# The order of the 64-row products in a gated-linear-attention layer: heads and chunks alternate on the TensorE array

## The chip, the cores and the metric

The kernel runs on one core of a Trainium2 chip. The metric is the device time of one execution in microseconds; lower is better. Three timed runs of the kernel before gave 604.95, 606.73 and 607.09 us (median 606.73). All views below come from one further execution, recorded by the hardware profiler.

## What is computed

One step of a hybrid block: adaLN-RMSNorm, a mixer with two branches (a gated linear recurrence, RG-LRU, and gated linear attention, GLA), a projection and residual, then a hierarchical mixture of 16 experts and a last norm. There are 640 tokens (512 latent ones, 128 of the prompt), 1024 channels, all in float32. The change touches the GLA part, which the reference writes as follows (4 heads of 64 key rows and 128 value columns, chunks of 64 tokens, a forward and a backward direction):

```python
def gla_scan(q, k, v, logg, s0):
    ...
    att = jnp.einsum('bhnid,bhnjd->bhnij', q * jnp.exp(b - b_ref), k * jnp.exp(b_ref - b))
    att = jnp.where(mask, att, 0.0)
    o_intra = jnp.einsum('bhnij,bhnjv->bhniv', att, v)
    q_in = q * jnp.exp(b)
    kv = jnp.einsum('bhnjd,bhnjv->bhndv', k * jnp.exp(b_last - b), v)
    decay = jnp.exp(b_last[:, :, :, 0, :])
    def step(s, inp):
        q_c, kv_c, d_c = inp
        o = jnp.einsum('bhid,bhdv->bhiv', q_c, s)
        return d_c[..., None] * s + kv_c, o
    ...
```

Three kinds of product come from it: the scores (`att`), the chunk states (`kv`) and the read-out (`o_intra` plus `o_inter`).

## The kernel before

Every engine has its own instruction list, written out by hand and tied together by semaphores; TensorE's list is the block under `@block.tensor`. Its results go to PSUM. Three places of 1024 floats (two banks each) form a ring, `ps`; each product takes the next place in a fixed list, `order`, and may start only when the product three places earlier has been taken out of PSUM by its reader. This wait is the last line of `start(name)` (L1098): `wait_taken(pe, ring[n - RING])`. `order` also names the reader of each product, A for ScalarE and D for VectorE, who serve them in that order; a second pair of banks, `ms`, holds products that stand aside from the ring, among them the turned keys `kT`.

Around the change TensorE does, for each of four groups g (a group is a direction s = g % 2 and a pair of heads tt = g // 2, which lie in the upper and the lower 64 rows of a tile):

- `kT{g}` (L1263): five transposes of the decayed keys, waiting for `kd_ready`.
- `at{g}0` and `at{g}1` (L1272), the scores of the two heads: for each of five 128-token tiles one product with 64 rows (the head's half of the rows, `rows_h`) and 128x128 outputs. The two heads go into two places of the ring. The change is here.
- `og{g}` (L1104, `project`), the first half of a 1024-deep projection to 128 x 640, which waits for its 512 KB tile of weights.
- `kvA{g}` and `kvB{g}` (L1291), the chunk states: products with 64 rows (the half that holds the chunk) and 64 output rows (the head), 20 in all, in which chunk and head alternate.
- the second half of `og{g}`.

In ring order this is at{g}0, at{g}1, og{g}, kvA{g}, kvB{g}, and again for g + 1. So at{g+1}0 takes the place of og{g}, which ScalarE empties (L897), and at{g+1}1 the place of kvA{g}, which VectorE empties. VectorE's list has, for each g: `scores(g)`, which takes both heads' scores through a mask (L1756; for odd g L1759 adds them to the sum of both directions); for g = 0 and 1 also `differences(g + 2)` (L1737, L1738) and `scale_qk(g + 2)` (L1743, L1744), with ScalarE's exponentials (L919 to L923) between them; then `carry(g)`, which runs the recurrence over the chunks of kvA (L1774, seven steps) and of kvB (L1782, L1783).

Then comes the read-out. TensorE does yl0, attend(0), yl1, attend(1), turn_o(0), yl2, attend(2), turn_o(1), yl3, attend(3), turn_o(2), attend(4), turn_o(3). `attend(t)` makes the 128 x 512 output of token tile t. For each head: one product of the scores with the values, with 128 rows and 128 columns (L1312), and up to four products of `qin` with the chunk states, with 64 rows (the head's half) and 64 output rows (the half of the chunk's tokens), for two chunks and two directions (L1322). The heads of a pair write into different banks (`hh * 512`). Tile 4 has two L1322 products per head, the others four. ScalarE takes the squares of each o{t} (L999) and their roots (L1001), VectorE the reciprocal and the scaling (L1815, L1820), TensorE turns the result (L1330, `turn_o`), and VectorE gates it (L1825). Between them ScalarE takes yl{t} through a gelu (L990). After that follow the output projection `mix` (L1386), the router and the experts (L1453, L1474).

Of the kernel before, what the change touches and what calls it, by code (L numbers as in the profile page):

```python
# [12 lines left out]
P = 128  # L13
EPS = 1e-6
GRID_W = 64
CHUNK = 64
# [4 lines left out]
def hybrid_step(nc, x_prompt, x_sample, state_lru, state_gla, c, c_ctx, ada_w, ada_b, norm1_g, w_in,  # L21
# [8 lines left out]
    NT = N // P  # L30
# [4 lines left out]
    HEADS, DK, DV = state_gla.shape[3:]  # L35
# [3 lines left out]
    NC = N // CHUNK  # L39
    SC = NS // CHUNK  # L40
# [22 lines left out]
    with ctx:  # L63
        def sb(name, shape, dt=F32):
            return ctx.enter_context(nc.sbuf_tensor(name, shape, dt))

        def sem(name):
            return ctx.enter_context(nc.semaphore(name))
# [14 lines left out]
        v = vtok[:, :].rearrange("p (t n) -> p t n", t=NT)  # L83
# [20 lines left out]
        qin = bcum  # L104
        softp = mixT[:, LC:, :]
        gt = tmp[:, 0:6 * N].rearrange("p (j n) -> p j n", j=6)
        attb = tmp[:, 6 * N:7 * N]
        att = tmp[:, 8 * N:12 * N].rearrange("p (h n) -> p h n", h=HEADS)
        o0 = 12 * N + LC * XLP
        NST = 8  # L110
        S = tmp[:, o0:o0 + 4 * NST * DV].rearrange("p (g c v) -> p g c v", g=4, c=NST)
# [7 lines left out]
        def state_slot(s, cn):  # L119

            return NST - 1 if cn >= SC else cn - 1 if s == 0 else cn
# [44 lines left out]
        sg0 = sb("sg0", [P, 4, DV])  # L166
# [126 lines left out]


        made = {name: n + 1 for n, (name, _) in enumerate(order)}
        for g in range(4):
            at_og = made[f"og{g}"]
# [10 lines left out]
        def product(name):  # L308
            if name in turned_keys:
                return ms[:, :, :].rearrange("p b n -> p (b n)")  # L310
            return ms[:, aside[name], :] if name in aside else ps[:, place[name] % RING, :]
# [20 lines left out]
        def weights(name):  # L332
            return wring[:, slot_of[name], :].rearrange("p (k n) -> p k n", k=KD)
# [21 lines left out]
        product_ready = sem("product_ready")  # L355
# [86 lines left out]
        at, off = [], 0  # L442
        for _, n in sm_parts:
            at.append(off)
            off += n
# [10 lines left out]
        def wait_tile(eng, name, i):  # L456
            eng.wait_ge(tile_in[i], 16 * (tiled[name][1] + 1))

        def count(name):

            n = [m for m, _ in order].index(name)
            who = order[n][1]
            return who, sum(w == who for _, w in order[:n + 1])

        def wait_taken(eng, name):
            who, n = count(name)
            eng.wait_ge(took[who], n)
# [615 lines left out]
        def _(pe):  # L1083
            mm = nc.tensor.matmul

            def start(name):

                if name in turned_keys:
                    wait_taken(pe, f"kT{int(name[2:]) - 1}" if name != "kT0" else "aTx")
                    return product(name)  # L1090
                if name in aside:
                    same = [m for m in aside if aside[m] == aside[name]]
                    if same.index(name):
                        wait_taken(pe, same[same.index(name) - 1])
                    return product(name)
                n = place[name]
                if n >= RING:
                    wait_taken(pe, ring[n - RING])  # L1098
                return product(name)
# [60 lines left out]
            def project(name, w, col, ks=range(KD)):  # L1160

                dst = start(name)
                for k in ks:
                    i = wide(dst, w[:, k, col:col + P], hT[:, k, :], k == 0, k == KD - 1)
                if k == KD - 1:
                    i.then_inc(product_ready, 1)
# [52 lines left out]
            dst = start("gd")  # L1219
            for k in range(KD):  # L1220
                r = 32 * (k % 4)
                for d, x in zip(halves(dst), halves(hT[:, k, :])):
                    i = mm(d[r:r + 2 * RANK, :], wgd[:, k, :], x, start=(k < 4), stop=(k >= 4), skip_group_check=True)
# [33 lines left out]
            for g in range(4):  # L1257
                r = 3 * (g % 2)
                tt = g // 2
                pe.wait_ge(kd_ready, g + 1)  # L1260
                dst = start(f"kT{g}")
                for t in range(NT):
                    i = nc.tensor.transpose(dst[:, t * P:(t + 1) * P], gt[:, r + 2, t * P:(t + 1) * P], ident[:, :])  # L1263
                i.then_inc(product_ready, 1)

                pe.wait_ge(qk_ready, g + 1)
                for hh in range(2):
                    dst = start(f"at{g}{hh}")
                    rows_h = slice(hh * DK, (hh + 1) * DK)
                    for t in range(NT):  # L1270
                        cols = slice(t * P, (t + 1) * P)
                        i = mm(dst[:, cols], gt[rows_h, r + 1, cols], gt[rows_h, r, cols], start=True, stop=True)  # L1272
                    i.then_inc(product_ready, 1)

                wait_tile(pe, "og", g)
                project(f"og{g}", weights("og"), g * P, range(0, KD // 2))
                wait_taken(pe, f"kT{g}")
                if g == 3:
                    pe.wait_ge(mod_out, 3)
                    nc.tensor.transpose(ms[0:8 * KD, 0, 0:P], A2[:, :, :].rearrange("p a k -> p (a k)"), ident[:, :]).then_inc(rowsT, 1)  # L1280
                    pe.wait_ge(lfin_ready, 8)
                    nc.tensor.transpose(ms[0:8, 0, P:2 * P], lfin[:, :], ident[:, :]).then_inc(lfinT, 1)
                for name, chunks in ((f"kvA{g}", range(SC)), (f"kvB{g}", range(SC, NC))):
                    dst = start(name)
                    for cn in chunks:
                        half = slice((cn % 2) * CHUNK, (cn % 2 + 1) * CHUNK)
                        col = (cn % 2) * 512 + (cn - chunks[0]) // 2 * DV
                        t = cn // 2
                        for hh in range(2):
                            h = 2 * tt + hh  # L1290
                            i = mm(dst[hh * DK:(hh + 1) * DK, col:col + DV],  # L1291
                                   kdT[g % 2][half, t * P + hh * DK:t * P + (hh + 1) * DK], v[half, t, h * DV:(h + 1) * DV],
                                   start=True, stop=True)
                    i.then_inc(product_ready, 1)
                project(f"og{g}", weights("og"), g * P, range(KD // 2, KD))
# [8 lines left out]
            def attend(t):  # L1304
                dst = start(f"o{t}")
                cols = slice(t * P, (t + 1) * P)
                for h in range(HEADS):
                    tt, hh = h // 2, h % 2
                    rows_h = slice(hh * DK, (hh + 1) * DK)

                    out = slice(hh * 512 + tt * DV, hh * 512 + (tt + 1) * DV)
                    mm(dst[:, out], att[:, h, cols], v[:, t, h * DV:(h + 1) * DV], start=True, stop=False, skip_group_check=True)  # L1312
                    parts = []
                    for cn in (2 * t, 2 * t + 1):
                        for s in range(2):
                            if cn >= SC and cn == (SC if s == 0 else NC - 1):
                                continue
                            first = cn == (0 if s == 0 else SC - 1)
                            parts.append((cn, s, sg0[rows_h, 2 * tt + s, :] if first else S[rows_h, 2 * tt + s, state_slot(s, cn), :]))
                    for n, (cn, s, state) in enumerate(parts):  # L1320
                        r = (cn % 2) * CHUNK
                        i = mm(dst[r:r + CHUNK, out], qin[rows_h, 2 * tt + s, cn * CHUNK:(cn + 1) * CHUNK], state, start=False,  # L1322
                               stop=(n == len(parts) - 1), skip_group_check=True)
                i.then_inc(product_ready, 1)

            def turn_o(t):
# [6 lines left out]
            for t in range(4):  # L1333
                if t:
                    wait_tile(pe, "yl", t)
                    project(f"yl{t}", weights("yl"), t * P)
                attend(t)
                if t:
                    turn_o(t - 1)
            attend(4)  # L1340
            turn_o(3)

# [81 lines left out]
            for n in range(2 * NT):  # L1424
                i = mm(ms[:, 0, 288:288 + 2 * NE], sel_a[:, n // NT, n % NT, :],  # L1425
                       gate_sel[:, n // NT, n % NT, :, :].rearrange("p h e -> p (h e)"), start=(n == 0),
                       stop=(n == 2 * NT - 1), skip_group_check=True)
# [65 lines left out]
            with pe.If(n_over > 0):  # L1493
# [4 lines left out]
                with pe.Fori(0, NOV) as i:  # L1498
                    with pe.If(n_over > i):
# [14 lines left out]
                        for half in range(2):  # L1514
                            for k in range(DC):
                                m = mm(ps[:, 2, half * 512:(half + 1) * 512], aT[:, 0, k, :], e2[0][:, k, half * 512:(half + 1) * 512],
                                       start=(k == 0), stop=(k == DC - 1))
# [686 lines left out]
```

## Time and profile before

| | |
|---|---|
| median of 3 runs | 606.73 us (604.95 to 607.09) |
| the profiled execution: its time | 606.16 us |
| its span, first to last instruction | 604.3 us |
| mean granted TensorE clock | 0.975 |
| TensorE busy | 554.6 us, 92% of the span |
| VectorE, ScalarE, GpSimd busy | 49%, 34%, 17% |
| scores (L1272) | 80 records, 187.1 to 230.3 us |
| read-out (L1312, L1322) | 40 and 144 records, 250.7 to 296.8 us |

Times inside the span count from its start. PE is TensorE's matmuls, PEld its weight loads, DVE VectorE, ACT ScalarE, POOL GpSimd, SP the queue that issues most transfers. A float32 product is recorded as two matmuls and two weight loads: the 40 score products stand as 80 records. A matmul's recorded duration contains its way through the array, so that neighbours overlap; the distance of starts, or the time that a chain gives to a run of them, is what a product costs.

### The profile page before, as it was taken

The numbers are of one execution on the slowest core, as the hardware profiler recorded it, in microseconds if no ns is written. First come the engines' busy times: TensorE is split into PE (matmuls) and PEld (weight loads), VectorE is DVE, ScalarE is ACT, GpSimd is POOL, SyncE is SP. The second block draws the span as 40 slices with busy tenths as digits, with TensorE's granted clock in tenths as the row PEclk, the third lists the DMA queues.
The fourth block names the chain that finished last, engine by engine and source line by source line (L and its number), as shares of the span: only waits on it lengthen the run. The fifth ranks groups of instructions, "written<-read, shape, count | busy, mean of one in ns | idle before, by whom it ended". The sixth has DMA issues, their size and how long they took to land.

```text
span 604.3 us, 6409 instructions
## 1 busy us (share of the span) xinstructions
PE 554.6 (92%) x2358; PEld 298.7 (49%) x2358; DVE 298.7 (49%) x592; ACT 203.3 (34%) x372; POOL 103.3 (17%) x113
## 2 busy tenths in 40 slices
PE   0899999999999999999999999699999999999970
PEld 0445545554346665566545555464454454454430
DVE  0532646948303764021344455515765576666671
ACT  5422289972412201533411122210000543443440
POOL 3000000001501220000000000040232454453332
PEclk9999999999999999999999999769999999999995
DMA  7977664118537802600019511179999999999411
GB/s 278 387 239 205 207 203 145 36 35 285 183 124 187 283 1 73 193 0 1 1 26 390 211 69 70 70 241 398 398 364 361 349 331 358 348 324 337 165 49 47
DMA packets 74418, 120.44 MB, mean 199 GB/s; under 512 B 13890, under 2 KB 31635, under 8 KB 74387
## 3 DMA queue, kind: packets, MB, share of 16 engines
q1 hardware_dynamic: 63880, 104.23, 49.7%
q0 software_dynamic: 10368, 15.75, 7.3%
q8 instruction: 19, 0.31, 0.2%
q14 instruction: 13, 0.10, 0.0%
q10 hardware_dynamic: 138, 0.04, 0.0%
HBM read 115.51 MB, written 26.51 MB: 235 GB/s over the span
## 4 chain that ended last, share of the span: by engine, by line
PE 85%; ACT 4%; DVE 3%; issue 1%; DMA 1%; POOL 0%; POOLq 0%; DVEq 0%
PE ps L1104 25%; PE ms L1453 18%; PE ps L1386 12%; PE ps L1474 9%; PE ps L1179 6%; PE ps L1436 2%; PE ps L1124 2%; PE ps L1322 2%; PE ms L1124 1%; PE ps L1272 1%; PE ms L1357 1%; PE ps L1312 1%; PE ps L1291 1%; PE ms L1425 1%; DMA wring<-in_w_in_dram 1%
## 5 line engine op out<-in xcount | busy, mean ns | idle before, releaser
L1104 PE MATMUL ps<-r,wring 128*128 128x512 f32 (+1 forms) x512 | 143.7, 436 | 1.6 <-ACT mixT L897 0.9
L1104 PEld LDWEIGHTS ps<-r,wring 128*128 128x128 f32 x512 | 79.0, 191 | 67.3 <-issue 66.1
L1386 PE MATMUL ps<-wring,mixT 128*128 128x512 f32 x160 | 72.1, 599 | 0.5 <-DVE tmp L1865 0.5
L1453 PE MATMUL ms<-wring,tmp 128*128 128x512 f32 x128 | 57.7, 593 | 1.3 <-DVE tmp L2044 1.3
L684 POOL DMA_INDIRECT mixT<-h_rows,slot_tok x16 | 19.6, 1224 | 192.6 <-DVE slot_tok L1972 178.8
L1386 PEld LDWEIGHTS ps<-wring,mixT 128*128 128x128 f32 x160 | 29.2, 190 | 32.0 <-issue 31.3
L1453 PEld LDWEIGHTS ms<-wring,tmp 128*128 128x128 f32 x128 | 23.6, 190 | 27.9 <-issue 26.3
L1179 PE MATMUL ps<-wring,r 128*128 128x512 f32 x80 | 35.6, 598 | 0.5 <-issue 0.5
L1043 ACT ACTIVATE tmp<-ms 128x256 f32<-128x256 f32 x16 | 6.1, 384 | 88.6 <-PE ms L1453 88.6
L2079 DVE TENSOR_TENSOR tmp<-ps,tmp 128x512 f32<-128x512 f32 x32 | 22.1, 691 | 16.8 <-PE ps L1474 16.8
L1453 PE MATMUL ms<-r,tmp 128*128 128x512 f32 x64 | 30.1, 617 | 0.0
L1054 ACT ACTIVATE tmp<-xres 128x512 f32<-128x512 f32 x24 | 15.1, 630 | 41.2 <-DVE xres L2083 41.2
L1453 PE MATMUL ms<-tmp 128*128 128x512 f32 x64 | 28.8, 592 | 0.0
L1474 PE MATMUL ps<-wring,gd 128*128 128x512 f32 x64 | 28.8, 592 | 0.0
L700 POOL DMA_INDIRECT residual_rows<-xres,back_row x16 | 16.4, 1024 | 69.4 <-DVE xres L2083 69.1
L1016 ACT ACTIVATE gd<-xres 128x512 f32<-128x512 f32 x10 | 6.3, 630 | 59.5 <-DVE xres L1869 59.5
L1179 PEld LDWEIGHTS ps<-wring,r 128*128 128x128 f32 x80 | 14.8, 190 | 19.9 <-issue 19.8
L2044 DVE COPY tmp<-ps 128x1024 f32<-128x1024 f32 x15 | 18.4, 1224 | 9.9 <-PE ps L1436 9.5
L2083 DVE TENSOR_TENSOR xres<-xres,tmp 128x512 f32<-128x512 f32 x32 | 22.1, 692 | 1.1
L2059 DVE COPY gd<-ps 128x256 f32<-128x256 f32 x16 | 6.8, 424 | 27.9 <-PE ps L1463 27.9
L2072 DVE SCALAR_TENSOR_TENSOR tmp<-qk,tmp 128x1024 f32<-128x1024 f32 x16 | 20.4, 1275 | 0.0
L1830 DVE TENSOR_TENSOR mixT<-mixT,gd 128x640 f32<-128x640 f32 x4 | 3.3, 825 | 34.5 <-ACT gd L990 34.5
(318 smaller groups left out, 825.1 us busy)
## 6 DMA issues: line engine op xcount, KB each, us to landing
wring<-in_ada_w_dram SPq DMA_DIRECT2D x12, 2048.0 KB, 11.9
wring<-in_exp_w_dram SPq DMA_DIRECT2D x8, 2048.0 KB, 24.8
wring<-in_w_in_dram SPq DMA_DIRECT2D x16, 512.0 KB, 4.9
r<-in_exp_w_dram SPq DMA_DIRECT2D x4, 2048.0 KB, 22.5
wring<-in_exp_w_dram SPq DMA_DIRECT2D x8, 1024.0 KB, 18.8
tmp<-in_exp_w_dram SPq DMA_DIRECT2D x4, 2048.0 KB, 22.5
wring<-in_w_out_dram SPq DMA_DIRECT2D x2, 2048.0 KB, 12.3
vtok<-in_exp_w_dram SPq DMA_DIRECT2D x4, 1024.0 KB, 17.0
```

Source lines behind the costliest of these rows:

```text
L684: pool.indirect_dma_start(gx[:, b, :], None, h2_d[:, :], rows_at(slot_tok[:, e:e + 1]), bounds_check=N - 1, oob_is_err=False).then_inc(gx_ ...
L700: pool.indirect_dma_start(xacc_d[:, :], rows_at(back_row[:, e:e + 1]), xr[:, u % 3, :], None, bounds_check=N - 1, oob_is_err=False).then_i ...
L1104: i = mm(d, lhsT, r, start=first, stop=last)
L1124: i = mm(dst[r:r + 32, 0:512], vec[:, k, :], w[:, k, :], start=(k < 4), stop=(k >= 4), skip_group_check=True)
L1179: i = mm(dst[:, 0:512], hT[:, k, t * P:(t + 1) * P], w[:, k, :], start=(k == 0), stop=(k == KD - 1))
L1386: i = mm(product(f"mx{t}")[:, half * 512:(half + 1) * 512], mixT[:, k, t * P:(t + 1) * P], w[:, k, :], start=(k == 0), stop=(k == KD - 1))
L1453: i = mm(ms[:, b, :], xgT[:, b, k, :], e13[u % 4][:, k, :], start=(k == 0), stop=(k == KD - 1))
L1474: i = mm(ps[:, 2, half * 512:(half + 1) * 512], aT[:, b, k, :], e2[u % 4][:, k, half * 512:(half + 1) * 512], start=(k == 0), stop=(k == D ...
L2044: V.tensor_copy(xgT[:, u % 2, :, :].rearrange("p k n -> p (k n)"), ps[:, 0, :]).then_inc(x_taken, 1)
L2072: link(stt(g2, rows[1][3], prompt[:, e:e + 1], rows[0][3], ALU.mult, ALU.add))
L2079: tt_(g2[:, cols], ps[:, 2, cols], g2[:, cols], ALU.mult).then_inc(y_taken, 1)
L2083: tt_(xr[:, u % 3, cols], xr[:, u % 3, cols], g2[:, cols], ALU.add).then_inc(z_half, 1)
```

## The change

In the scores both places of the ring are asked for first, then the two heads alternate from tile to tile. In the read-out the two heads of a pair go together: both 128-row products first, then for each direction and chunk the product of one head and that of the other. The number, sizes and operands of the products stay the same.

```diff
@@ -1264,13 +1264,15 @@
                 pe.wait_ge(qk_ready, g + 1)
-                for hh in range(2):
-                    dst = start(f"at{g}{hh}")
-                    rows_h = slice(hh * DK, (hh + 1) * DK)
-                    for t in range(NT):
-                        cols = slice(t * P, (t + 1) * P)
-                        i = mm(dst[:, cols], gt[rows_h, r + 1, cols], gt[rows_h, r, cols], start=True, stop=True)
-                    i.then_inc(product_ready, 1)
+
+                dsts = [start(f"at{g}{hh}") for hh in range(2)]
+                for t in range(NT):
+                    cols = slice(t * P, (t + 1) * P)
+                    for hh in range(2):
+                        rows_h = slice(hh * DK, (hh + 1) * DK)
+                        i = mm(dsts[hh][:, cols], gt[rows_h, r + 1, cols], gt[rows_h, r, cols], start=True, stop=True)
+                        if t == NT - 1:
+                            i.then_inc(product_ready, 1)
@@ -1304,23 +1306,23 @@
             def attend(t):
                 dst = start(f"o{t}")
                 cols = slice(t * P, (t + 1) * P)
-                for h in range(HEADS):
-                    tt, hh = h // 2, h % 2
-                    rows_h = slice(hh * DK, (hh + 1) * DK)
-
-                    out = slice(hh * 512 + tt * DV, hh * 512 + (tt + 1) * DV)
-                    mm(dst[:, out], att[:, h, cols], v[:, t, h * DV:(h + 1) * DV], start=True, stop=False, skip_group_check=True)
-                    parts = []
-                    for cn in (2 * t, 2 * t + 1):
-                        for s in range(2):
-                            if cn >= SC and cn == (SC if s == 0 else NC - 1):
-                                continue
-                            first = cn == (0 if s == 0 else SC - 1)
-                            parts.append((cn, s, sg0[rows_h, 2 * tt + s, :] if first else S[rows_h, 2 * tt + s, state_slot(s, cn), :]))
-                    for n, (cn, s, state) in enumerate(parts):
-                        r = (cn % 2) * CHUNK
-                        i = mm(dst[r:r + CHUNK, out], qin[rows_h, 2 * tt + s, cn * CHUNK:(cn + 1) * CHUNK], state, start=False,
-                               stop=(n == len(parts) - 1), skip_group_check=True)
+                for tt in range(HEADS // 2):
+
+
+                    outs_of = [slice(hh * 512 + tt * DV, hh * 512 + (tt + 1) * DV) for hh in range(2)]
+                    for hh in range(2):
+                        mm(dst[:, outs_of[hh]], att[:, 2 * tt + hh, cols], v[:, t, (2 * tt + hh) * DV:(2 * tt + hh + 1) * DV],
+                           start=True, stop=False, skip_group_check=True)
+                    parts = [(s, cn) for s in range(2) for cn in (2 * t, 2 * t + 1)
+                             if not (cn >= SC and cn == (SC if s == 0 else NC - 1))]
+                    for n, (s, cn) in enumerate(parts):
+                        first = cn == (0 if s == 0 else SC - 1)
+                        c = (cn % 2) * CHUNK
+                        for hh in range(2):
+                            rows_h = slice(hh * DK, (hh + 1) * DK)
+                            state = sg0[rows_h, 2 * tt + s, :] if first else S[rows_h, 2 * tt + s, state_slot(s, cn), :]
+                            i = mm(dst[c:c + CHUNK, outs_of[hh]], qin[rows_h, 2 * tt + s, cn * CHUNK:(cn + 1) * CHUNK], state,
+                                   start=False, stop=(n == len(parts) - 1), skip_group_check=True)
                 i.then_inc(product_ready, 1)
```

## Rows read from the trace of the kernel before

**Rows 1.** The page: busy shares, and the chain that ended last by engine.

```profile
PE 554.6 (92%) x2358; PEld 298.7 (49%) x2358; DVE 298.7 (49%) x592; ACT 203.3 (34%) x372; POOL 103.3 (17%) x113
...
PE 85%; ACT 4%; DVE 3%; issue 1%; DMA 1%; POOL 0%; POOLq 0%; DVEq 0%
```

**Rows 2.** The chain in order of time, 185 to 242 us (start us, us, what).

```profile
185.74 4.09 DMA wring<-in_w_in_dram
...
194.47 1.25 PE ps L1291 x40
...
228.46 2.13 PE ps L1272 x20
```

**Rows 3.** The same chain: attend(1), and the start of yl2 behind turn_o(0).

```profile
263.56 0.22 PE ps L1312 x2
263.79 0.59 PE ps L1322 x8
264.38 0.42 PE ps L1312 x2
...
267.99 8.65 PE ps L1104 x32
```

**Rows 4.** Stretches within L1272: us, PE busy (records), PEld busy (loads), PEclk, DMA share, GB/s.

```profile
201.13:202.22 1.09, 1.09 (x10) 1.09 (x10) 1.00 1.04 385
214.78:215.87 1.09, 1.09 (x10) 1.09 (x10) 1.00 0.05 15
228.46:229.55 1.09, 1.09 (x13) 1.09 (x14) 1.00 0.02 8
```

**Rows 5.** Timeline of DVE, 199 to 226 us (start us, us, engine, line, what).

```profile
199.91 2.27 DVE L1774 SCALAR_TENSOR_TENSOR tmp<-tmp,dec,ps 128x128 f32<-128x128 f32 x6
...
202.67 0.86 DVE L1756 COPY_PREDICATED tmp<-mask,ps 128x640 f32<-128x640 uint32 x1
...
210.38 0.83 DVE L1743 TENSOR_TENSOR tmp<-tmp,qk 128x640 f32<-128x640 f32 x1 [2.68 <-ACT tmp L923]
...
213.58 2.27 DVE L1774 SCALAR_TENSOR_TENSOR tmp<-tmp,dec,ps 128x128 f32<-128x128 f32 x6
...
223.28 2.27 DVE L1774 SCALAR_TENSOR_TENSOR tmp<-tmp,dec,ps 128x128 f32<-128x128 f32 x6
```

**Rows 6.** Stretches of 0.04 us: within L1291, then within L1322 (columns as rows 4).

```profile
194.39:194.43 0.04, 0.03 (x4) 0.03 (x4) 1.00 1.09 256
...
251.02:251.06 0.04, 0.03 (x2) 0.04 (x2) 1.00 0.82 231
```

**Rows 7.** Timeline of PE, attend(4) and turn_o(3), 294 to 298 us.

```profile
294.31 0.44 PE L1322 MATMUL ps<-tmp 64*64 64x128 f32 x4
294.67 0.49 PE L1312 MATMUL ps<-vtok,tmp 128*128 128x128 f32 x2
...
297.46 0.63 PE L1330 MATMUL ps<-ident,tmp 128*128 128x128 f32 x4 [0.36 <-DVE tmp L1820]
```

**Rows 8.** Timeline of ACT behind yl1 and around attend(3).

```profile
264.96 0.70 ACT L990 ACTIVATE gd<-ps 128x640 f32<-128x640 f32 x1
...
291.12 0.70 ACT L990 ACTIVATE gd<-ps 128x640 f32<-128x640 f32 x1
293.62 0.28 ACT L999 ACTIVATE tmp<-ps 128x128 f32<-128x128 f32 x1 [1.80 <-PE ps L1322]
```

**Rows 9.** Stretches of PE, 386 to 412 us: us, PE busy (records), PEclk, DMA share, GB/s.

```profile
386.00:388.00 2.00, 0.29 (x3) 0.65 0.15 61
388.00:402.00 14.00, 9.85 (x40) 0.50 0.52 177
...
410.20:411.60 1.40, 0.08 (x2) 1.00 1.05 413
```

**Rows 10.** What PE waited for: us in total, times, longest us.

```profile
PE ms L1365 <- DVE tmp L1914: 3.3, 1, 3.3
...
PE ps L1104 <- DMA wring<-in_w_in_dram: 0.7, 1, 0.7
```

## The prediction

> **What bounds the kernel now.** I read first the page: TensorE is busy for 92% of the span, and 85% of the chain that ended last is its own work [rows 1]. So time that TensorE loses or saves reaches the end, unless something else comes due in its place. I then read the chain in order of time over the two stretches that the change touches. It shows how long each run of products holds the chain, and where the chain leaves TensorE: a transfer before the first og [rows 2], and ScalarE and VectorE behind attend(3) [rows 7, 8]. Last I looked at stretches and timelines for what runs at the same time in the array and who frees the places of the ring.
>
> **What an order is worth in the array.** Before, the four L1322 products of a head lie in one half of the rows and in two halves of the columns. Two records start within 0.04 us [rows 6], so two corners of the array already work at once, and 8 records take 0.59 us [rows 3]. The chunk states (L1291) go round all four corners: four records start within 0.04 us [rows 6], and 40 take 1.25 us [rows 2]. That is 4 records per corner in 0.59 and 10 per corner in 1.25: 0.66 us for 6 more rounds, 0.11 per round whatever the number of corners. Two rounds, in attend(4), take 294.67 - 294.31 = 0.36 [rows 7], on the same line (0.59 - 2 x 0.11 = 0.37).
>
> **Read-out, tiles 0 to 3.** A head behind another costs 0.42 for its L1312 pair of records, which needs a change from and to the 64-row form, and 0.59 for its 8 records, together 1.01. A pair that follows no change of form costs 0.22 [rows 3]. Two heads together will cost 0.42 for the first L1312 product, 0.22 for the second, which follows directly, and 0.59 for 16 records in four rounds over four corners: 1.23 against 2.02, a saving of 0.79. In the first pair of heads of a tile it is 1.03 against 1.82, the same 0.79. Two pairs in four tiles: 8 x 0.79 = 6.3 us. The unknown is whether products that add to earlier ones go round as those of L1291, which do not add, do. The bounds: nothing better than four rounds, 0.59; at worst the pace of two corners, 0.11 for two records, so that 16 take 0.59 + 4 x 0.11 = 1.03 and a pair of heads saves 0.35, 2.8 us in all. I take 0.59, since both neighbouring rows agree on 0.11 a round and the L1322 records that add do keep it on two corners.
>
> A rule speaks against it. The row first: four records within 0.04 us, 40 in 1.25, which is 0.031 for each [rows 2, 6]. The Trainium skill, TensorE: Matmul & The Clock Gate (section "Back-to-back issue gap"), says that without the hardware's decoder every matmul costs the sequencer about 62 ns, which then bounds small ones. As an estimate from that page of the Trainium skill, 16 records would take 0.99 and the read-out would save 3.1 us rather than 6.3, a time of 603.8. The trace disagrees with it for L1291.
>
> **What lies behind the read-out.** Savings of tiles 0 to 2 reach the next projection directly. yl2 will start at 267.99 - 1.58 = 266.41 and needs the place of yl1, which ScalarE has emptied at 265.66 [rows 3, 8]. The gelu of yl3 ends at 291.82, and ScalarE then idles until 293.62 [rows 8]. After the change attend(3) ends 1.58 earlier, its squares can start at 293.62 - 1.58 = 292.04, 0.22 behind the gelu: just no wait. Behind attend(3) the chain is squares, root, scaling, turning, from 293.62 to 297.46 [rows 7, 8]; it moves as a whole. attend(4) lies beside that chain. Each of its two pairs goes from 2 x 0.79 to 0.42 + 0.22 + 0.37 = 1.01, some 1.1 less together, but turn_o(3) already waits 0.36 for VectorE [rows 7], so this buys nothing: the wait becomes some 1.5. Sum for the read-out: -6.3.
>
> **Scores.** Each head has 10 records at 0.11 and a first one at 0.2; alternating, both heads take the time of one, some 1.1. But the groups differ.
>
> - g = 0: its 20 records, from 187.1, would be through some 0.8 earlier. og0 waits for its weights, which land by 185.74 + 4.09 = 189.83, and TensorE already waits 0.7 for them [rows 2, 10]. The transfers are issued at 185.74, before the change acts, so they don't move. 0.
> - g = 1 and 2: here a wait moves. In the first 1.09 us only 10 records begin, those of the first head; in g = 3 it is 13, since the second head starts before the first is through [rows 4]. In g = 1 and 2 the second head waits: its place holds kvA of the group before, and VectorE's recurrence on that ends at 199.91 + 2.27 = 202.18, in g = 2 at 213.58 + 2.27 = 215.85 [rows 5], when the 11th record can begin. The change asks for both places before the first product, so the first head, 1.1 us of work that used to lie in front of this wait, now stands behind it. g = 1: start 202.2 instead of 201.13 [rows 4], both heads in 1.1 plus 0.2, so og1 at 203.5 as before. 0 gained.
> - What is late next: VectorE took at10 at 202.67 [rows 5], but now it is complete only with at11, at some 203.3 plus 0.35 to be seen, 203.7. It is 1.0 late, and its list from there has no room: masks, differences, ScalarE's exponentials, scale_qk, recurrence follow each other, the one stop of 2.68 being ScalarE's part of that same chain [rows 5]. So kvA1 is emptied at 216.85, not 215.85, g = 2 ends 1.0 later: +1.0. No transfer hangs on it; the og tiles are there, and SP waits for og's end only to refill for yl, long needed later. GpSimd's steps for g = 3 follow the exponentials, also 1.0 later, but kT3, which needs them, comes only at 227.
> - g = 3: VectorE is free, the recurrence on kvA2 is through at 225.55 [rows 5], in future 226.6, before 229. The two heads shrink from 2.13 [rows 2] to 1.3 or so: -0.8.
>
> Bounds of the scores: -3.0 if the places were free (g = 1, 2 save 1.1 each, g = 3 0.8), +1.8 if VectorE's delay were 1.8 (its two masks and sums of g = 1 queued once more behind the wait) and g = 3 gained nothing. I take 0 + 0 + 1.0 - 0.8 = +0.2.
>
> **The sum.** -6.3 + 0.2 = -6.1. The profiled execution took 606.16 us (span 604.3 and 1.9 around it), so it would take 600.1. The median of the runs shown is 0.57 above it: 606.73 - 6.1 = 600.6, which I forecast. No change of DMA or of instruction counts adds a term, and everything behind mix moves forward as one piece, with the issue of expert weights, since those are triggered by TensorE's and VectorE's own steps.
>
> **Rivals.**
>
> 1. *The pace stays that of two corners*, because the sequencer can't feed four when products add into PSUM. Read-out saves 2.8: 606.73 - 2.8 + 0.2 = 604.1. Against it: L1291 goes round four corners, with two banks, just as here [rows 6]. For it: no row shows four corners with adding. (The 62 ns of the Trainium skill's page would come to nearly the same time, by another reason.) Chance 0.08.
> 2. *The waits in the scores don't bind*, so the heads overlap in g = 1 and 2 as well: 606.73 - 6.3 - 3.0 = 597.4. Against it: the 10 records and VectorE's 202.18 and 215.85 [rows 4, 5]. Chance 0.03.
> 3. *Slower: the clock falls in a new pause.* The change makes pauses on TensorE: 1.1 more before the scores of g = 1 and 2, and 1.5 before turn_o(3), amid small products. The trace shows one fall, at about 386.6, with PE idle for 3.3 [rows 9, 10], and 0.50, which is 1.2 of 2.4 GHz, is held until some time after 402, 16 us or more. A stretch like that full of products costs about 16 x 0.5 = 8: 606.73 - 6.1 + 8 = 608.6, and 617 with two. It decides if a pause of 1.5 is long enough for a fall; a pause of 1.3 at 410.2 left the clock at 1.00 [rows 9]. Chance 0.05.
> 4. *The change does nothing*, since the array pulls later products forward by itself. It does so across the heads in g = 3, by three records. In the read-out a 128-row product stands between the heads, and it never reaches over that. Chance 0.01, 606.7.
>
> The rest, 0.03, is for a stop of ScalarE before o3 or a slip of a few tenths per pair that I don't see.
>
> **Chances and range.** A measurement of this kernel can tell about 0.5% from no change, 3.0 us: faster is below 603.7. The forecast has 0.80, with its own range of 599.4 to 601.9 (0.1 per pair of heads is 0.8, and the three runs spread over 2.1). The range reaches from a part of the score gain on one side to the pace between two and four corners on the other: 599.0 to 603.8. Faster: 0.80 + 0.03 + a little of case 1 and the rest, 0.86. Same: most of case 1, case 4, a short fall of the clock, 0.10. Slower by over 0.5%, above 609.8: case 3 with two falls, 0.02, and most of the rest, 0.04.
>
> **What would show it.** In the changed kernel four L1322 records start within 0.04 us; the chain shows 16 records in 0.59 and L1312 as x4 in 0.64 (0.44 at first). attend(3) takes 1.58 less from its first L1312 to turn_o(2); turn_o(3) waits about 1.5 for L1820. The scores of g = 1 begin near 202.2 and those of g = 2 near 216.9, each right behind L1774, all 20 records in about 1.3; L1756 of g = 1 starts near 203.7. PEclk stays 1.00 from 180 to 300. I am wrong if 16 records take over 0.8, if the scores of g = 1 start at 201.1, or if PEclk falls there.

## The result, and the profile after

The changed kernel takes 599.49 us (median of 4 runs, 599.43 to 602.29) against 606.50 for the kernel before: a ratio of 0.990, interval 0.987 to 0.993. Forecast were 600.6 us and a range of 599.0 to 603.8. Six more runs beside later experiments had a median of 599.74. The profiled execution took 599.51 us, its span 597.8, 6.5 less than before.

The page: busy shares, as [rows 1].

```profile
PE 543.4 (91%) x2358; PEld 290.9 (49%) x2358; DVE 298.6 (50%) x592; ACT 203.1 (34%) x372; POOL 103.2 (17%) x113
```

The chain of the changed kernel in order of time (start us, us, what), its read-out part, as [rows 3].

```profile
250.97 0.45 PE ps L1314 x4
251.41 0.60 PE ps L1324 x16
252.01 0.64 PE ps L1314 x4
252.65 0.60 PE ps L1324 x16
...
287.50 1.14 ACT tmp L999 x8
...
291.33 0.63 PE ps L1332 x4
```

A corner, here and below, is a quarter of TensorE's array: one half of its rows by one half of its columns. 16 records with 64 rows hold the chain for 0.60 us, as long as 8 did before (0.59), and the four records with 128 rows for 0.64 (0.45 where no change of form precedes). A tile takes 2.29 against 3.84. In the first 0.04 us four records start, where two did [rows 6]. The columns of the stretch are those of [rows 4]:

```profile
251.34:251.38 0.04, 0.04 (x4) 0.04 (x4) 1.00 0.31 90
```

The timeline of TensorE shows the scores of the four groups and the turning behind attend(4), as [rows 7].

```profile
186.82 1.39 PE L1273 MATMUL ps<-tmp 64*128 64x128 f32 x20
189.73 4.59 PE L1104 MATMUL ps<-r,wring 128*128 128x512 f32 x16 [1.52 <-DMA wring<-in_w_in_dram]
...
202.06 1.39 PE L1273 MATMUL ps<-tmp 64*128 64x128 f32 x20 [1.43 <-DVE tmp L1776]
203.38 4.59 PE L1104 MATMUL ps<-r,wring 128*128 128x512 f32 x16
...
216.77 1.39 PE L1273 MATMUL ps<-tmp 64*128 64x128 f32 x20 [2.48 <-DVE tmp L1776]
218.09 4.59 PE L1104 MATMUL ps<-r,wring 128*128 128x512 f32 x16
...
229.29 1.39 PE L1273 MATMUL ps<-tmp 64*128 64x128 f32 x20 [0.29 <-issue]
...
242.08 4.34 PE L1104 MATMUL ps<-r,wring 128*128 128x512 f32 x14 [0.89 <-ACT mixT L897]
...
291.33 0.63 PE L1332 MATMUL ps<-ident,tmp 128*128 128x128 f32 x4 [1.47 <-DVE tmp L1822]
291.99 0.67 PE L1388 MATMUL ps<-wring,mixT 128*128 128x512 f32 x1
```

Every group's 20 records take 1.39, and yet nothing is won before yl0. After g = 0, TensorE waits longer for the weights of og0 (1.52 instead of 0.66); g = 1 and 2 now wait for VectorE. The chain that ended last shows it too: from 190.01 to 216.64 it runs through VectorE's list and ScalarE's exponentials between, and, of TensorE's work, only through the scores of g = 1:

```profile
201.57 0.36 DVE tmp L1776
201.93 0.14 issue
202.06 1.41 PE ps L1273 x20
203.47 0.86 DVE tmp L1758
```

VectorE's timeline, as [rows 5], shows why g = 2 is late:

```profile
199.65 2.26 DVE L1776 SCALAR_TENSOR_TENSOR tmp<-tmp,dec,ps 128x128 f32<-128x128 f32 x6
...
203.45 0.87 DVE L1758 COPY_PREDICATED tmp<-mask,ps 128x640 f32<-128x640 uint32 x1 [0.95 <-PE ps L1273]
...
214.36 2.27 DVE L1776 SCALAR_TENSOR_TENSOR tmp<-tmp,dec,ps 128x128 f32<-128x128 f32 x6
```

L1756 of before is L1758 here: 203.45 instead of 202.67. The first L1776 run is itself 0.26 earlier, so against it the mask is 1.04 late, and so is the next recurrence.

To take out such small shifts ahead of the change I measure two stretches in each kernel's profiled execution: from the start of og0 to that of yl0 (scores), and from the start of attend(0) to that of mix (read-out). A clock fall is a stretch in which the granted clock of TensorE is 0.50 (1.2 of 2.4 GHz). The kernel before, run again beside the experiments, had medians of 606.40 to 606.48; experiment 10 has one run only.

| kernel | og0 to yl0 | attend(0) to mix | median, us |
|---|---|---|---|
| before | 52.11 | 47.41 | 606.5 |
| changed | 52.35 | 41.18 | 599.5 |
| 1 read-out alone | 52.19 | 41.18 | 599.8 |
| 2 scores alone | 54.28, a clock fall in it | 47.41 | 607.2 |
| 3 both places first | 55.76, a clock fall in it | 47.44 | 609.2 |
| 4 pairs, head by head | 52.33 | 41.32 | 600.6 |
| 5 pairs, old order | 52.09 | 41.38 | 599.8 |
| 6 changed, again | 55.62, a clock fall in it | 41.19 | 599.7 |
| 7 apart in g = 1, 2 | 51.21 | 41.18 | 599.1 |
| 8 four heads, two start marks | 51.39 | 39.76 | 598.0 |
| 9 four heads, one start mark | 51.33 | 39.76 | 597.9 |
| 10 corner by corner | 51.38 | 45.57 | 604.9 |

The change costs 0.24 us in the first stretch and saves 6.23 in the second, 6.0 together; behind mix the profiled execution is another 0.4 shorter, in the router's pauses. The 0.24 is no larger than the spread of single profiled executions: the four kernels with the old order of the scores (before, 1, 4, 5) have 52.09 to 52.33 in the first stretch.

### The profile page after: what moved, and what is told of

It reads as the page before. It is cut to its first block, busy times and chain, and to the rows that moved or that the text cites. A ratio compares the mean times of both kernels' runs of the same rounds, so it can differ in the third digit from the quotient of the medians.

```text
span 597.8 us, 6409 instructions
## 1 busy us (share of the span) xinstructions
PE 543.4 (91%) x2358; PEld 290.9 (49%) x2358; DVE 298.6 (50%) x592; ACT 203.1 (34%) x372; POOL 103.2 (17%) x113
## 4 chain that ended last, share of the span: by engine, by line
PE 57%; DVE 5%; ACT 2%; issue 2%; POOL 0%; POOLq 0%; DVEq 0%
PE ms L1455 19%; PE ps L1388 12%; PE ps L1104 9%; PE ps L1476 9%; PE ps L1438 2%; PE ms L1359 1%; DVE tmp L1776 1%; PE ps L1324 1%; PE ps L1314 1%; PE ms L1427 1%; DVE tmp L1746 1%; PE ps L1273 1%; PE ps L1350 1%; PE ps L1465 1%; PE ps L1293 0%
```

## Experiments

**1, read-out alone.** `attend` as changed, the scores' loop as before.

> The change in the read-out alone; the scores go head by head as before. My theory (four corners of the array share the time of one, and the read-out carries the whole gain): mix (L1386) starts 6.3 us earlier than before, time 606.5 - 6.3 = 600.2, the scores as before (x20 in 2.16, 2.47, 2.49, 2.13). Rival (the alternating scores bring a good part, some 3 us): 603.2.

599.75 us (ratio 0.989, 0.987 to 0.991), and mix starts as far behind attend(0) as in the changed kernel, 41.18 us. The read-out carries the whole gain.

**2, scores alone.** The scores' loop as changed, `attend` as before.

> The change in the scores alone; the read-out head by head as before. My theory (the wait for the second place moves in front of both heads in g = 1 and 2 and eats what alternating saves): yl0 starts within 0.2 us of the kernel before, og2 about 0.9 later, time 606.6 (within 0.5). Rival (scores gain in every group in which no transfer is waited for): -3.0, 603.5.

607.22 us, ratio 1.001 (1.000 to 1.002): no gain. The profiled execution is 2.2 us longer up to yl0, though, not 0.2. Stretches of TensorE in it (us, PE busy (records), PEclk, DMA share, GB/s):

```profile
214.00:217.40 3.40, 0.92 (x9) 1.00 0.00 0
217.40:220.80 3.40, 3.40 (x21) 0.50 0.02 5
220.80:222.00 1.20, 1.20 (x6) 1.00 0.00 0
```

The scores of g = 2 start at 217.40 behind the pause for VectorE, and for 3.4 us TensorE has half its clock: 1.7 us lost. 54.28 - 1.7 = 52.6 is 0.5 above the kernel before, where at most 0.2 was expected. In five of the ten runs the mean clock is 0.972 or 0.973; the other five, at 0.975, have a median of 606.55, which is what was expected (606.6). The fall is a side effect that I had priced wrongly; more of it below.

**3, the wait alone.**

```diff
-                for hh in range(2):
-                    dst = start(f"at{g}{hh}")
+                dsts = [start(f"at{g}{hh}") for hh in range(2)]
+                for hh in range(2):
+                    dst = dsts[hh]
```

> The wait alone: the kernel before, but both places of the ring are asked for ahead of the first head's products; the heads still go one behind the other. My theory: in g = 1 the products start at 202.2 instead of 201.1, and VectorE gets at10 1.1 later; in g = 2 they start about 216.9 and end 2.1 later than before; g = 0 and g = 3 as before. yl0 and the time +2.1 us: 608.6. Rival (VectorE's list has room, so the lateness is not handed on): only +1.1, and the scores of g = 2 start no later than 215.9: 607.6.

609.18 us, ratio 1.0041 (1.0025 to 1.0057). In the chain, the scores of g = 2 and what releases them:

```profile
213.91 0.27 DVE tmp L1775
...
216.12 0.36 DVE tmp L1775
216.48 0.14 issue
216.61 2.13 PE ps L1273 x20
218.74 5.56 PE ps L1104 x13
```

og1 stands 14.63 us behind og0 (before 13.65), og2 29.34 (before 27.33): +1.0 and another +1.0. The lateness is handed on, as expected; in the trace the rival is out. Up to yl0 it is 55.76, less 1.7 for a clock fall 54.1: +1.95 for 2.1 expected. The small rest is that both heads' scores, once both places are free, overlap by themselves (2.13 for the 20, as in g = 3 of the kernel before, not 2.49). The whole times alone would not decide it: in 8 of the 10 runs the mean clock is 0.970 to 0.972, and the two others took 607.70 and 606.87 us, nearer to the rival's 607.6. The profiled execution also has a second fall of 3.4 us at 300.8, behind turn_o(3), whose wait of 0.4 is that of the kernel before.

**4, pairs, but head by head.**

```diff
-                    for n, (s, cn) in enumerate(parts):
-                        ...
-                        for hh in range(2):
+                    for hh in range(2):
+                        for n, (s, cn) in enumerate(parts):
+                            ...
```

> In the read-out the two 128-row products of a pair stand together as in the change, but the 64-row ones follow head by head (order of directions and chunks as in the change), so that only two corners are at work but for the seam; the scores as before. My theory: a pair of heads takes 0.42 + 0.22 + 1.03 less some 0.1 at the seam = 1.6 instead of 2.02, so 8 x 0.4 = 3.2 us less than before: 603.3, and 3.1 us more than the read-out change alone. Rival (all of the gain is the fewer changes of form between 128 and 64 rows): the same as the read-out change alone, 600.2.

My theory missed: from attend(0) to mix it takes 41.32 us, 0.14 more than the changed kernel and not 3.1. Four records, now of one head after the other in the list, start within 0.04 us (columns as in [rows 4]):

```profile
251.50:251.54 0.04, 0.04 (x4) 0.04 (x4) 1.00 0.55 166
```

(Its median of 600.6 rests on runs from 598.7 to 601.2; the profiled one has a clock fall of 3.4 us that begins during turn_o(3), behind a wait of 1.5.) So alternating the heads isn't what brings four corners to work. That opened the next experiment.

**5, pairs, old order.** As 4, and `parts` in the order of the kernel before (even chunk twice, odd chunk twice).

> As the fourth experiment (the 128-row products of a pair together, 64-row products head by head, scores as before), but the 64-row products of each head in the order of the kernel before as well: even chunk twice, odd chunk twice. So each head's products come two on one corner, then two on the next. New theory (the array looks ahead and starts a later product on a free corner by itself; the 128-row product between two heads was what it could not pass): 16 records still in 0.6 to 0.75 us, attend(0) to mix as with the read-out change, within 1 us of it, 599.5 to 601. The prediction's theory (the order sets how many corners work): 16 records in 1.0, about 603.5.

599.76 us, ratio 0.989 (0.988 to 0.990). The chain, and a stretch at the start of the first 64-row records:

```profile
250.96 0.45 PE ps L1312 x4
251.40 0.62 PE ps L1322 x16
252.02 0.64 PE ps L1312 x4
252.66 0.62 PE ps L1322 x16
```

```profile
251.32:251.38 0.06, 0.05 (x4) 0.05 (x4) 1.00 0.28 77
```

The 64-row products are here in exactly the old order within each head; only the second head's 128-row product has moved in front of them. Four corners start within 0.06 us all the same, and 16 records take 0.62. The array starts later products on free corners by itself, over products that still wait for theirs. What it did not pass in the kernel before was a 128-row product. Whether that is so because such a product needs all four corners or because of the change of form was not separated.

**10, how far it looks.** From kernel 9 below, the 64-row products of a tile go corner by corner, four in a row on each:

```diff
+                for c in (0, CHUNK):
+                    for hh in range(2):
+                        ...
+                        for tt in range(HEADS // 2):
+                            ...
+                            for n, (s, cn) in enumerate(here):
```

> As the ninth, but the 16 products with 64 rows of a tile go corner by corner: four products in a row on each of the four corners. Theory (each corner holds one running and one waiting product; a third for the same corner stops the list): the second corner starts when the first begins its third product, 0.44 us in, the others 0.88 and 1.32 in; a tile's 32 records take 1.3 us longer than in the ninth (2.2 from first to last instead of 0.9), tiles 0 to 2 lose 1.3 each and tile 3 too: +5 us, 603. Rival (the array looks ahead without such a bound): four corners at once and the time of the ninth. Second rival (it looks only a fixed number of records ahead, as far as in the fifth experiment): between the two.

```profile
250.53 0.89 PE ps L1320 x8
251.42 2.49 PE ps L1333 x32
253.92 1.17 PE ps L1104 x3
```

The one run took 604.88 us (expected: 603), with a clock fall of 3.4 us in it that begins during turn_o(3). 2.49 us for 32 records (the chain), against 1.03 in kernel 9, and 5.8 us more from attend(0) to mix (expected: 5). Stretches of 0.49 us within L1333, from the first record on (us, PE busy (records), PEld busy (loads), PEclk, DMA share, GB/s):

```profile
251.35:251.84 0.49, 0.49 (x4) 0.49 (x5) 1.00 0.00 0
251.84:252.33 0.49, 0.49 (x10) 0.49 (x9) 1.00 0.00 0
```

Four records, two products, run alone on the first corner for 0.49 us; only when its third product begins does the second corner start. That fits one running and one waiting product per corner, and a third that stops the list. A look-ahead over a fixed number of records does not fit: here the 9th record of the list starts only after 0.49 us, while in experiment 5 the 9th and the 13th, the first ones of the second head's two corners, start within 0.06. The bound also fits the scores of before. There a head's five products all use the same half of the rows, and the second head begins 0.75 us in, with the fourth product of the first, which is why 13 records and not 10 start in the first 1.09 us [rows 4]. And it says why the old order of the read-out was harmless: no head puts more than two products on a corner.

**6, the changed kernel again**, beside 7 and 8.

> The changed kernel once more, beside the next two on the same chip: 599.5, with some runs 1.5 to 3 us above it in which the mean clock is below 0.974 (a short fall of the clock in one of the new pauses), as in two of the runs so far.

599.74 us (599.11 to 603.93). Two of the six runs stand above the rest, 601.65 and 603.93; the second is 4.2 above the median, more than the 3 expected. The profiled one is the 603.93. Stretches of TensorE in it (columns as in 2):

```profile
214.00:217.00 3.00, 1.11 (x8) 1.00 0.00 0
217.00:218.00 1.00, 0.41 (x4) 0.63 0.00 0
218.00:224.00 6.00, 6.00 (x26) 0.50 0.01 3
```

It is the same pause in front of the scores of g = 2. The clock falls at its end, and stays at half for nearly 7 us. PEclk below 1.00 between 180 and 300 is one of the signs by which the prediction would call itself wrong; the first profiled execution of the changed kernel did not show it, this one does.

**7, apart in g = 1 and 2.** The scores' loop of before under `if g in (1, 2)`, the changed one otherwise.

> The changed kernel, but in g = 1 and 2 the scores go head by head again, each head behind its own wait; g = 0 and 3 alternate. My theory (asking for the second place early costs 0.9 us in g = 2 and nothing in g = 1): og2 starts about 0.9 earlier against g = 0 than in the changed kernel, g = 3 keeps its 0.7, so the time is 599.5 - 0.9 = 598.6, and the pause before the scores of g = 2 is gone, and with it falls of the clock there. Rival (nothing is won, since VectorE's chain comes due elsewhere): 599.5.

599.13 us, ratio 0.988 (0.986 to 0.990), beside 0.990 (0.988 to 0.992) for the changed kernel on the same chip: right in sign, not settled by the times. The trace settles it: 51.21 us from og0 to yl0, 1.14 less than changed and 0.90 less than before, and no pause for VectorE:

```profile
213.89 0.71 ACT mixT L897
214.61 0.14 issue
214.74 2.49 PE ps L1273 x20
217.24 2.14 PE ps L1104 x6
```

Its profiled execution has a clock fall of 3.4 us at 291.2, behind the pause before turn_o(3).

**8 and 9, all four heads of a tile together.** On top of 7, the 128-row products of both pairs first; in 9 also:

```diff
-                           start=True, stop=False, skip_group_check=True)
+                           start=(tt == 0), stop=False, skip_group_check=True)
```

> As the seventh, and in the read-out all four 128-row products of a tile first, then the 32 records with 64 rows. My theory (a change of form costs 0.2 in and 0.2 out, less the 0.1 to 0.2 that a run of products starts with anyway): a tile takes 0.9 + 0.6 + 0.44 = 1.9 instead of 2.3, 0.4 less; tiles 0 to 2 give 1.2 us, tile 3 only 0.25, since ScalarE's gelu of yl3 ends 0.25 before its squares of o3 start now. Sum -1.4 against the seventh: 597.2. Rival (the cost of a pair is not in the change of form): 598.6.

> As the eighth, but only the first of the two 128-row products that go into one PSUM bank is marked as the start of a sum; the second one (tt = 1) is not. Theory (a start mark clears what the bank remembers of written sums, also of the neighbour's columns, so that in the eighth the sums of tt = 0 lost their first product): same instructions, same time as the eighth, 598.0, 0.36 us less per tile than the pair order. Rival: unmarked, the second product adds to old contents of its columns.

8 took 597.97 us (expected 597.2, its rival 598.6), 9 597.90 (ratio 0.986, 0.984 to 0.988). The medians don't decide between 8's two theories; the distance from attend(0) to mix does, below. In 8 two of the kernel's four outputs are off by as much as their size (relative errors 1.05 and 1.03), in 9 none, and the start mark is the only difference between the two. So in 8 the sums of the pair tt = 0 lose their 128-row product: the second start mark, on neighbouring columns of the same bank, made the next product overwrite. The Trainium skill, PSUM — Partial Sum Buffer (section "Terms", row "Zero region"), says so: what one start mark clears is the whole 2 KiB bank in the quadrants it writes. The runs agree. The chain of 9 around attend(0) and behind yl3:

```profile
249.84 0.89 PE ps L1320 x8
250.74 1.03 PE ps L1332 x32
251.77 1.28 PE ps L1104 x4
```

```profile
284.35 0.70 ACT gd L990
285.05 1.03 ACT tmp L999 x8
```

A tile takes 1.92 instead of 2.29, 0.37 less; attend(0) to mix takes 39.76 in 8 and in 9, 1.42 less (1.4 expected). As expected, tile 3 now ends before ScalarE's gelu of yl3, and the squares of o3 start where the gelu ends. 9 is the fastest kernel here, 8.5 us below the kernel before. In its four runs the mean clock stayed at 0.974 to 0.975.

## Why the prediction was right, and where not

- *Read-out, -6.3*: measured -6.23. A tile takes 1.55 less (said: 1.58): two runs of eight records and two changes of form are gone (0.60 for 16 records, 0.64 and 0.45 for four). The tail behind attend(3) moved as one piece, attend(4) bought nothing, turn_o(3) waits 1.47 (said: 1.5), and ScalarE had 0.25 to spare before o3 (said: 0.22).
- *What made the four corners work* was named wrongly. The prediction let the order "go round" the corners and took the heads' alternation for the cause; its case 4 saw that a 128-row product stands between the heads, and went no further. Experiments 4 and 5 show that moving this one product is all of it, 41.3 and 41.4 us against 41.18; alternating adds 0.1 to 0.2. That the sum came right all the same is partly luck: the change makes both moves at once. For an order without the alternation, experiment 4, the same reasoning gave 603.3 where 600.6 was measured.
- *The 62 ns a matmul of the Trainium skill* (TensorE: Matmul & The Clock Gate, section "Back-to-back issue gap") did not bind: in the trace of the changed kernel 16 records start in 0.4 us.
- *Scores, +0.2*: measured +0.24, which by itself is within the spread of the first stretch; what is clear of it are the steps, and they are the ones given. g = 1 started behind VectorE's recurrence at 202.06 (said: 202.2), VectorE's next mask was 1.0 late, og2 came 1.03 later against og0, g = 3 gave 0.8 back. Experiments 2 and 3 show that this is the wait's doing; 7 gets it back.
- *The clock*, case 3 with 0.05: mis-sized in both terms. The clock falls more often, and for less. In the changed kernel 3 of 10 runs (601.65, 602.29, 603.93 us) have a mean clock of 0.969 to 0.971, while all 37 runs of the kernel before that stood beside the experiments have 0.974 or more. I took the price of a fall from the one of 17 us in the trace; those seen at the new pauses last 3.4 or nearly 7 us and cost, at half the clock, up to 1.7 or 3.4. Only the 603.93 was seen in a trace; for the other two the mean clock speaks. Experiment 3, whose waits in front of the scores are shorter (1.7 at most, against 2.5), has a low mean clock in 8 of 10 runs, so the length of the wait alone does not order the kernels.
- *The sum*: -6.0 up to mix for -6.1. The median moved by 7.0, the second series by 6.7; the rest lies behind mix and within the spread of the runs.

## What to carry to other kernels

Before reordering small products for concurrency, look for what separates them: here a product of full size between two groups cost 1.5 us a tile, while the orders of experiments 4 and 5 cost 0.1 to 0.2 us in the whole read-out, since the array, as far as these runs show, passes over up to one waiting product per corner by itself. In these runs order mattered where three or more products in a row use the same corner or half of the rows, as in the scores and in experiment 10, where it cost 1.46 us a tile. And when two results are interleaved, both of their buffers are asked for before the first product: look who frees the later one, and give it the work that used to cover the wait.

## What was not expected of the hardware

- With 64-row, 64-column float32 products of two records each, what the runs show fits an array that keeps one running and one waiting product per corner and starts later ones on other corners, within 0.06 us for four (experiments 5 and 10). The bound of one waiting is read from two patterns (10: the second corner after 0.49 us; the old scores: the second head after 0.75); other sizes were not tried.
- At the end of pauses of 1.5 to 2.5 us next to small products, or up to 2.3 us behind them, TensorE's clock sometimes fell from 2.4 to 1.2 GHz for 3.4 us or nearly 7 us (experiments 2, 3, 4, 6, 7, 10), in some executions of a kernel and not in others. In experiment 3 it fell once more where the pause was only 0.4. What decides in which executions was not tried.
